# A two-block sequence model on one core: input turned before its modulation, sums shared by two engines, last norm on statistics operations

## The chip, the cores and the metric

The kernel runs on one core of a Trainium2 chip. The metric is the device time of one execution in microseconds (us). Three timed runs of the kernel before gave 2133.89 us as their median (2132.24 to 2136.08). A profile was taken of one more execution, which lasted 2128.42 us.

The engines are named as in the profile: PE is TensorE (PEld its weight loads), DVE is VectorE, ACT is ScalarE, POOL is GpSimd, SP is SyncE, which here only issues transfers.

## The reference

A sequence of 1024 tokens of 1024 features (float32) goes through two blocks. Only the two ends matter here.

```
# first block, its start
mod = silu(c) @ w_mod + b_mod               # c: (1, 1024), w_mod: (1024, 3072)
shift, scale, gate = split(mod, 3)
h = rms_norm(x, norm_g) * (1 + scale) + shift
proj = h @ w_in                             # then a state space mixer, sparse attention,
...                                         # gates, output projection, final rms_norm
# second block: projections, dilated attention, a chunked scan, two RMS norms, then its end
out = mix @ w_out                           # mix: (1024, 2048), w_out: (2048, 1024)
y = layer_norm(alpha * x + out, ln_g, ln_b) # mean and variance over 1024 features
```

In both blocks the tokens stand in 8 tiles of 128. A product with `h` wants the features on the partitions, so `x`, which arrives with tokens on the partitions, has to be transposed ("turned") on PE.

## The kernel before, in words

Every engine has its own instruction stream, written out by hand in one function, and waits on semaphores by count. SP loads the weights in 34 loads of 2 MB into two halves of one buffer `W`; a load starts when its half has been used. PE multiplies them in units of one PSUM bank, and this chain of units fills most of the span.

**The start.** SP issues, in this order, the parameters `pk`, the first half of `x` (tiles 0 to 3), the constants `ck` (they hold the identity for the transposes), `mods[0]`, the second half of `x`, `mods[1]` to `mods[3]`, and then the first two weight loads. The four `mods` are 2 MB each: 512 columns of `w_mod` for all 1024 rows of `c`; two of them land in `W` (slots 0 and 1), two in `hT`. The load of weights 0 waits until `mods[0]` has been summed (`s_macc`), the load of weights 1 until `mods[1]` has.

- DVE, function `modulation(m)` (L1731 to L1741): one multiply and seven multiply-adds of 128x512 sum `silu(c)[k] * w_mod[k]` over the eight slices k into `mod_sum[m]`. The sum over the 128 partitions is PE's: four products of 128 columns of `mod_sum[m]` with a column of ones (L1067), each a result of one column.
- ACT squares the tiles of `x` with an accumulated sum and takes the root (L1419, L1423); DVE, function `normalise(half)`, scales four tiles (L1751).
- The order on DVE is modulation 0, normalise 0, modulation 1, normalise 1, modulation 2, modulation 3. Then come three small operations that make the scale `sc1` and the shift `shf` (L1760 to L1762, the last of them signals `s_mod`).
- PE transposes 16 pieces ("turns", each four 128x128 transposes into one bank, L1057): six of them before the modulation products, ten behind them, on six banks. A turned piece is read out of PSUM by DVE (even, L1767) or ACT (odd, L1430), and this read applies `sc1` and `shf`; so none can be read before `s_mod`, and PE gets no bank for the seventh.
- The first unit of the load "small" (L868) waits for all 16 pieces. From there on PE has work.

**The end.** The last two loads, woA0 and woA1, give 16 units of 24 products each. DVE adds each unit to the row tile `res` (L2227). Behind each unit of woA1, the function `row_norm` finishes the tile before it: ACT sums the row (L1613), DVE makes the negative mean (L2212), ACT sums the squares about it (L1615), DVE makes the variance (L2214), ACT the root (L1618), and DVE the reciprocal (L2217) and three passes of 128x1024 (L2218, L1631, L2220). POOL issues the store of each tile (L770).

## Time and profile before

| what | us |
|---|---|
| median of three runs | 2133.89 |
| the profiled execution | 2128.42 |
| its span, first to last instruction | 2126.6 |
| PE busy in it | 1967.8 (93%) |
| DVE busy in it | 1157.7 (54%) |
| first unit of "small" starts on PE | 57.59 |
| last product of PE ends | 2106.13 |
| last pass of DVE ends | 2120.84 |

The page of the profile gives the shares; the times of the two ends are read from the timeline. Between 57.59 and 2106.13 PE is nearly always busy or waited for; ahead of it lies the preparation of `h`, behind it the last layer norm and its stores. The granted clock of PE is printed as a share of 2.4 GHz, so 0.50 is 1.2 GHz.

### The profile page before, as it was taken

To read this page: it belongs to the slowest core of one execution; us is meant where nothing else is said; L and a number is where in the kernel's file an instruction comes from. 1 tells how busy PE (TensorE), PEld (TensorE's weight loads), DVE (VectorE), ACT (ScalarE), POOL (GpSimd) and SP (SyncE) were. 2 spreads that over 40 slices of the span, in tenths; PEclk is the share of its full clock that TensorE was granted. 3 is DMA by queue.
4 is the path that set the end of the run, shared out by engine and by line. 5 is a ranking of instruction groups with operands and counts; after the bars stand their busy time and mean duration, and the time that the engine had idled before them with its cause. 6 is when DMAs were issued, how large, how long until landed. Compare 5 with 4: busy or idle time off the path is not lost.

```text
span 2126.6 us, 27616 instructions
## 1 busy us (share of the span) xinstructions
PE 1967.8 (93%) x10964; PEld 982.9 (46%) x10964; DVE 1157.7 (54%) x2320; ACT 757.1 (36%) x1345; POOL 613.2 (29%) x630
## 2 busy tenths in 40 slices
PE   2999889998999999989999899899999999999896
PEld 2443344454444455534444566544444444444542
DVE  6418999999995456422545688620233333332516
ACT  2413444314312866213321344331233333333503
POOL 0022415544446002478311322511101222022240
PEclk8999999999999999999999999999999999999998
DMA  8110111022311002331311100211111011100301
GB/s 336 40 45 25 50 40 50 21 85 75 129 79 69 37 11 85 139 119 40 128 40 40 40 1 1 79 40 40 41 41 41 1 41 41 41 10 32 120 20 79
DMA packets 18225, 127.10 MB, mean 60 GB/s; under 512 B 1744, under 2 KB 1744, under 8 KB 12848
## 3 DMA queue, kind: packets, MB, share of 16 engines
q1 hardware_dynamic: 12720, 97.57, 12.1%
q0 software_dynamic: 5376, 27.76, 3.3%
q8 instruction: 87, 1.43, 0.3%
q14 instruction: 42, 0.34, 0.0%
HBM read 106.45 MB, written 18.87 MB: 59 GB/s over the span
## 4 chain that ended last, share of the span: by engine, by line
PE 75%; DVE 14%; ACT 4%; POOL 3%; DMA 2%; issue 2%; SPq 0%; DVEq 0%; POOLq 0%; ACTq 0%
PE ps L871 48%; PE ps L868 7%; DVE arena L1631 3%; POOL arena L570 2%; PE ps L986 1%; PE ps L1223 1%; PE ps L921 1%; PE ps L963 1%; PE ps L969 1%; PE ps L908 1%; PE ps L1243 1%; PE ps L1088 1%; PE ps L936 1%; DMA W<-in_mods 1%; DVE arena L1847 1%
## 5 line engine op out<-in xcount | busy, mean ns | idle before, releaser
L871 PE MATMUL ps<-hT,W 128*128 128x512 bf16 x3456 | 812.3, 389 | 23.0 <-DVE arena L2150 7.2
L871 PEld LDWEIGHTS ps<-hT,W 128*128 128x128 bf16 x3456 | 327.6, 97 | 465.6 <-issue 34.9
L579 POOL TENSOR_TENSOR W<-W 128x512 bf16<-128x512 f32 x216 | 235.9, 1131 | 459.6 <-DMA W<-in_loads 458.3
L871 PE MATMUL ps<-W,arena 128*128 128x512 bf16 x1152 | 262.4, 388 | 8.8 <-DVE W L2016 6.2
L570 POOL TENSOR_TENSOR arena<-arena 128x512 f32<-128x512 f32 (+1 forms) x80 | 139.7, 1746 | 196.4 <-ACT arena L1569 126.4
L1409 ACT ACTIVATE arena<-arena,small 128x128 f32<-128x128 f32 (+9 forms) x192 | 114.1, 641 | 198.9 <-DVE small L1721 181.9
L871 PEld LDWEIGHTS ps<-W,arena 128*128 128x128 bf16 x1152 | 111.1, 97 | 158.1 <-DVE W L2016 6.7
L1402 ACT ACTIVATE arena<-arena,small 128x128 f32<-128x128 f32 (+9 forms) x192 | 122.8, 640 | 122.8 <-DVE small L1710 87.3
L868 PE MATMUL ps<-arena,W 128*128 128x512 f32 (+1 forms) x320 | 142.0, 598 | 0.9 <-DVE arena L1767 0.9
L871 PE MATMUL ps<-arena,W 128*128 128x512 bf16 x576 | 132.3, 391 | 5.4 <-POOL arena L631 4.4
L1710 DVE CUSTOM_DVE_ANT_0 arena<-ps,arena 128x256 f32<-128x256 f32 (+7 forms) x128 | 62.1, 518 | 123.8 <-PE ps L969 109.4
L741 POOL TENSOR_TENSOR small<-small 128x1024 f32<-128x1024 f32 x7 | 14.0, 1999 | 342.2 <-ACT small L1393 342.2
L1859 DVE TENSOR_SCALAR_CACHE_REDUCE small<-arena,small 128x768 bf16<-128x768 f32 (+2 forms) x93 | 101.7, 1143 | 1.1
L868 PEld LDWEIGHTS ps<-arena,W 128*128 128x128 f32 (+1 forms) x320 | 57.8, 185 | 77.9 <-issue 75.2
L871 PEld LDWEIGHTS ps<-arena,W 128*128 128x128 bf16 x576 | 55.7, 97 | 81.6 <-POOL arena L631 4.9
L871 PE MATMUL ps<-W,hT 128*128 128x512 bf16 x384 | 89.5, 388 | 0.0
L1342 ACT ACTIVATE arena<-ps 128x512 f32<-128x512 f32 x48 | 28.3, 597 | 138.2 <-PE ps L871 74.8
L1653 DVE CUSTOM_DVE_ANT_0 arena<-ps,arena 128x128 f32<-128x128 f32 (+7 forms) x64 | 45.9, 755 | 56.7 <-PE ps L921 35.9
L1683 DVE COPY arena<-ps 128x384 f32<-128x384 f32 (+2 forms) x64 | 26.3, 453 | 86.7 <-PE ps L986 46.1
L1686 DVE COPY arena<-ps 128x256 f32<-128x256 f32 (+1 forms) x64 | 30.8, 481 | 73.5 <-PE ps L989 73.5
L1640 DVE COPY arena<-ps 128x512 f32<-128x512 f32 (+3 forms) x96 | 49.0, 551 | 39.4 <-PE ps L936 39.4
L1846 DVE MAX8 small<-arena 128x8 f32<-128x384 f32 (+2 forms) x96 | 66.4, 692 | 2.1
(321 smaller groups left out, 2673.7 us busy)
## 6 DMA issues: line engine op xcount, KB each, us to landing
W<-in_loads SPq DMA_DIRECT2D x34, 2048.0 KB, 7.6
gates_scratch<-arena SPq DMA_DIRECT2D x32, 256.0 KB, 2.0
arena<-gates_scratch POOLq DMA_DIRECT2D x2, 4096.0 KB, 15.4
arena<-in_x SPq DMA_DIRECT2D x2, 2048.0 KB, 13.8
W<-in_mods SPq DMA_DIRECT2D x2, 2048.0 KB, 18.4
hT<-in_mods SPq DMA_DIRECT2D x2, 2048.0 KB, 28.8
arena<-in_x POOLq DMA_DIRECT2D x1, 4096.0 KB, 13.5
x_scratch<-arena POOLq DMA_DIRECT2D x8, 512.0 KB, 8.7
```

The source lines that it names most:

```text
L570: return nc.gpsimd.tensor_tensor(o, a, b, ALU.mult)
L579: last = nc.gpsimd.tensor_tensor(low(v), v, high(v), ALU.subtract)
L868: last = mm(o, left, right, start=(k == 0), stop=(k == steps - 1))
L871: last = mm(o, left[:, :, a], right[:, :, b], start=(k == 0 and (a, b) == PRODUCTS[0]), stop=(k == steps - 1 and (a, b) == PRODUCTS[-1]))
L1402: A(t, t, ACT.Exp, bias=mneg4[:, (n % 2) * 2 + x:(n % 2) * 2 + x + 1], scale=-1.0, accum_out=den[:, (n % 2) * 2 + x:(n % 2) * 2 + x + 1]). ...
L1409: A(t, t, ACT.Copy, scale=rden[:, (n % 2) * 2 + x:(n % 2) * 2 + x + 1]).then_inc(sems["scaled"], 1)
L1631: return V.tensor_tensor(o, a, b, ALU.mult)
L1640: V.tensor_copy(tiles["cols"][g % 2][x][:, 0:nb * P], ps[:, 6 + x, 0:nb * P]).then_inc(sems["copied"], 1)
L1653: V.tensor_tensor_reduce(tiles["rows"][n % 2][x][:, 0:keys], ps[:, 2 + 2 * x:4 + 2 * x, :].rearrange("p a b -> p (a b)")[:, 0:keys], bias_ ...
L1710: V.tensor_tensor_reduce(at2["rows"][n % 2][x][:, 0:window(i)], ps[:, 2 + at_, 0:window(i)], bias_of(items[n], x), 1.0, BIG, ALU.add, ALU.min,
L1846: link(V.max(mx, sc_at(i)))
L1859: last = V.tensor_scalar(junk[b], sc_at(i), levels[b], None, ALU.is_ge, ALU.add, accum_out=count3[:, b:b + 1])
```

## The change

SP issues the first half of `x`, then `pk`, the second half of `x`, `ck`, the four `mods` and the weights. The input is normalised, turned and copied raw out of PSUM by ACT alone, over seven banks, before any modulation; when `sc1` and `shf` are there, DVE and ACT apply them in SBUF, one 128x1024 piece for each k, and the first unit of "small" waits for its pieces one by one. Of each `mods[m]`, DVE sums 256 columns as before, and PE takes the other 256: for two column tiles, eight accumulating products of a 128x128 weight tile with one column of `silu(c)`. The loads of weights 0 and 1 wait for PE's products (`s_mcol`). In the last norm, statistics operations on DVE (one bn_stats behind each unit, one bn_aggr for each row) give mean and variance, ACT keeps only the root, and two fused passes take the place of three. SP issues the stores.

```
             def load(n):
                 ...
-                    sp.wait_ge(s_macc, n + 1)
+                    sp.wait_ge(s_mcol, n + 1)
...
+            nc.sync.dma_start(XR0[:, 0:4, :], x[0:512].rearrange("(t p) d -> p t d", p=P)).then_inc(s_x[0], 16)
             nc.sync.dma_start(pk[:], params).then_inc(s_par, 16)
-            nc.sync.dma_start(XR0[:, 0:4, :], x[0:512].rearrange("(t p) d -> p t d", p=P)).then_inc(s_x[0], 16)
+            nc.sync.dma_start(XR0[:, 4:8, :], x[512:1024].rearrange("(t p) d -> p t d", p=P)).then_inc(s_x[1], 16)
             nc.sync.dma_start(ck[:], consts).then_inc(s_con, 16)
-            nc.sync.dma_start(mod_weights(0), mods[0]).then_inc(s_modw[0], 16)
-            nc.sync.dma_start(XR0[:, 4:8, :], x[512:1024].rearrange("(t p) d -> p t d", p=P)).then_inc(s_x[1], 16)
...
+            for m in range(4):
+                nc.sync.dma_start(mod_weights(m), mods[m]).then_inc(s_modw[m], 16)
...
+            for t in range(NT):
+                sp.wait_ge(s_ln[2], t + 1)
+                nc.sync.dma_start(out[t * P:(t + 1) * P, :], res[:, t, :]).then_inc(s_out, 16)
+            sp.wait_ge(s_out, 16 * NT)
...
-            for t in range(NT):
-                pool.wait_ge(s_ln[5], t + 1)
-                nc.gpsimd.dma_start(out[t * P:(t + 1) * P, :], res[:, t, :]).then_inc(s_out, 16)
-            pool.wait_ge(s_out, 16 * NT)
...
                 for (cols, lhs, rhs), span in spans:
                     for k in span:
+                        if (name, i) == ("small", 0):
+                            pe.wait_ge(s_hta if k % 2 else s_htv, k // 2 + 1)
...
-                if n >= 6:
-                    pe.wait_ge(s_hta if n % 2 else s_htv, (n - 6) // 2 + 1)
+                if n >= 7:
+                    pe.wait_ge(s_xt_read, n - 6)
...
-            for n in range(6):
+            for n in range(16):
                 turn_input(n)
+            pe.wait_ge(s_csil, 1)
             for m in range(4):
+                pe.wait_ge(s_modw[m], 16)
+                w = mod_weights(m).rearrange("p (k n) -> p k n", k=KD)
+                for ct in range(2, 4):
+                    for k in range(KD):
+                        mm(ps[:, 0, 4 * m + ct:4 * m + ct + 1], w[:, k, ct * P:(ct + 1) * P], csil[:, k:k + 1],
+                           start=(k == 0), stop=(k == KD - 1))
                 pe.wait_ge(s_macc, m + 1)
-                for ct in range(4):
+                for ct in range(2):
                     last = mm(ps[:, 0, 4 * m + ct:4 * m + ct + 1], mod_sum[m][:, ct * P:(ct + 1) * P], ones[:, 0:1],
                               start=True, stop=True)
-            last.then_inc(s_mcol, 1)
-            for n in range(6, 16):
-                turn_input(n)
-            pe.wait_ge(s_htv, 8)
-            pe.wait_ge(s_hta, 8)
+                last.then_inc(s_mcol, 1)
             pe.wait_ge(s_mod, 1)
+            pe.wait_ge(s_xt_read, 16)
             units("small")
...
+            for n in range(16):
+                k, half = turned(n)
+                act.wait_ge(s_xt, n + 1)
+                A(h_whole[k][:, half * 512:half * 512 + 512], ps[:, 1 + n % 7, :], ACT.Copy).then_inc(s_xt_read, 1)
             A(dts, par("ldt"), ACT.Exp).then_inc(s_prm, 1)
             act.wait_ge(s_mod, 1)
-            for n in range(1, 16, 2):
-                k, half = turned(n)
-                act.wait_ge(s_xt, n + 1)
-                A(h_whole[k][:, half * 512:half * 512 + 512], ps[:, 2 + n % 6, :], ACT.Identity, scale=sc1[:, k:k + 1],
-                  bias=shf[:, k:k + 1]).then_inc(s_hta, 1)
+            act.wait_ge(s_xt_read, 16)
+            for k in range(1, KD, 2):
+                A(h_whole[k], h_whole[k], ACT.Identity, scale=sc1[:, k:k + 1], bias=shf[:, k:k + 1]).then_inc(s_hta, 1)
...
             for t in range(NT):
-                act.wait_ge(s_free, FIRST["woA1"] + t + 1)
-                ...
-                junk = row_junk[t % 2]
-                A(junk, res[:, t, :], ACT.Copy, accum_out=ss[:, t:t + 1]).then_inc(s_ln[0], 1)
-                act.wait_ge(s_ln[1], t + 1)
-                A(junk, res[:, t, :], ACT.Square, bias=nmu[:, t:t + 1],
-                  accum_out=ss2[:, t:t + 1]).then_inc(s_ln[2], 1)
-                act.wait_ge(s_ln[3], t + 1)
-                A(rss[:, t:t + 1], rss[:, t:t + 1], ACT.Sqrt).then_inc(s_ln[4], 1)
+                act.wait_ge(s_ln[0], t + 1)
+                A(rss[:, t:t + 1], rss[:, t:t + 1], ACT.Sqrt).then_inc(s_ln[1], 1)
...
-                link(V.tensor_scalar(mod_sum[m], w[:, 0, :], csil[:, 0:1], None, ALU.mult))
+                link(V.tensor_scalar(mod_sum[m], w[:, 0, 0:256], csil[:, 0:1], None, ALU.mult))
                 for k in range(1, KD):
-                    ins = V.scalar_tensor_tensor(mod_sum[m], w[:, k, :], csil[:, k:k + 1], mod_sum[m], ALU.mult, ALU.add)
+                    ins = V.scalar_tensor_tensor(mod_sum[m], w[:, k, 0:256], csil[:, k:k + 1], mod_sum[m], ALU.mult, ALU.add)
...
-            modulation(0)
             normalise(0)
-            modulation(1)
             normalise(1)
-            modulation(2)
-            modulation(3)
-            dve.wait_ge(s_mcol, 1)
+            for m in range(4):
+                modulation(m)
+            dve.wait_ge(s_mcol, 4)
...
-            for n in range(0, 16, 2):
-                ...
+            dve.wait_ge(s_xt_read, 16)
+            for k in range(0, KD, 2):
+                V.tensor_scalar(h_whole[k], h_whole[k], sc1[:, k:k + 1], shf[:, k:k + 1], ALU.mult, ALU.add).then_inc(s_htv, 1)
...
             def row_norm(t):
-                ...
+                row, mean, root = res[:, t, :], row_mean[:, t, 0:1], inv_ln[:, t:t + 1]
+                link(V.bn_aggr(row_mean[:, t, :], row_stats[:, t].rearrange("p c n -> p (c n)")))
+                V.tensor_scalar(root, row_mean[:, t, 1:2], NORM_EPS / ALPHA ** 2, None, ALU.add).then_inc(s_ln[0], 1)
+                V.scalar_tensor_tensor(row, row, mean, lng, ALU.subtract, ALU.mult)
+                dve.wait_ge(s_ln[1], t + 1)
+                link(V.reciprocal(root, root))
+                V.scalar_tensor_tensor(row, row, root, lnb, ALU.mult, ALU.add).then_inc(s_ln[2], 1)

             for u in range(FIRST["woA0"], len(UNITS)):
                 ...
                 V.scalar_tensor_tensor(v, ps[:, unit_bank(u), :], inv[:, t:t + 1], v, ALU.mult, ALU.add).then_inc(s_free, 1)
+                dve.wait_ge(s_free, u + 1)
+                link(V.bn_stats(row_stats[:, t, c, :], v))
                 ...
-                if name == "woA1" and t >= 1:
-                    row_norm(t - 1)
-            row_norm(7)
+                if c:
+                    row_norm(t)
```

Where the instructions of an engine now stand is shown at three places. PE at the very start, before: 24 transposes, 16 products with ones, the other 40 transposes, and the unit "small" (72x512). A fp32 product is one row here and two records in the trace; a transpose is one of both.

```order
L1057 MATMUL ps<-ck,arena 128x128 x24
L1067 MATMUL ps<-ck,arena 128x1 x16
L1057 MATMUL ps<-ck,arena 128x128 x40
L868 MATMUL ps<-arena,W 72x512 x16
L868 MATMUL ps<-arena,W 128x512 x16
```

PE at the same place after the change; L1071 are the new products with `silu(c)`, L1075 those with ones:

```order
L1058 MATMUL ps<-ck,arena 128x128 x64
L1071 MATMUL ps<-small,W 128x1 x16
L1075 MATMUL ps<-ck,arena 128x1 x2
L1071 MATMUL ps<-small,W 128x1 x16
L1075 MATMUL ps<-ck,arena 128x1 x2
L1071 MATMUL ps<-small,hT 128x1 x16
L1075 MATMUL ps<-ck,arena 128x1 x2
L1071 MATMUL ps<-small,hT 128x1 x16
L1075 MATMUL ps<-ck,arena 128x1 x2
L869 MATMUL ps<-arena,W 72x512 x16
```

All 64 transposes have moved ahead of the modulation; between them and "small" there now stand 72 products with one column instead of 40 transposes.

DVE at the start, before: L1735 and L1737 are `modulation`, L1747 to L1751 `normalise`.

```order
L1735 TENSOR_SCALAR arena<-W,small 128x512
L1737 SCALAR_TENSOR_TENSOR arena<-W,small,arena 128x512 x7
L1747 TENSOR_SCALAR small<-small 128x4
L1749 RECIPROCAL small<-small 128x4
L1751 TENSOR_SCALAR arena<-arena,small 128x1024 x4
```

DVE after, from its first scaling of `x` on (L1746 to L1750 are `normalise`, L1734 and L1736 `modulation`):

```order
L1746 TENSOR_SCALAR small<-small 128x4
L1748 RECIPROCAL small<-small 128x4
L1750 TENSOR_SCALAR arena<-arena,small 128x1024 x4
L1746 TENSOR_SCALAR small<-small 128x4
L1748 RECIPROCAL small<-small 128x4
L1750 TENSOR_SCALAR arena<-arena,small 128x1024 x4
L1734 TENSOR_SCALAR arena<-W,small 128x256
L1736 SCALAR_TENSOR_TENSOR arena<-W,small,arena 128x256 x7
```

Both halves of `x` come first, and the sums behind them are half as wide.

DVE in the last stage, one row tile before (from the unit's read to the last pass of the tile before it):

```order
L2227 SCALAR_TENSOR_TENSOR arena<-ps,small,arena 128x512
L2212 TENSOR_SCALAR small<-small 128x1
L2214 TENSOR_SCALAR small<-small 128x1
L2217 RECIPROCAL small<-small 128x1
L2218 TENSOR_SCALAR arena<-arena,small 128x1024
L1631 TENSOR_TENSOR arena<-arena 128x1024
L2220 TENSOR_TENSOR arena<-arena 128x1024
```

One row tile after:

```order
L2219 SCALAR_TENSOR_TENSOR arena<-ps,small,arena 128x512
L2221 BN_STATS small<-arena 128x6
L2206 BN_AGGR small<-small 128x2
L2207 TENSOR_SCALAR small<-small 128x1
L2208 SCALAR_TENSOR_TENSOR arena<-arena,small 128x1024
L2210 RECIPROCAL small<-small 128x1
L2211 SCALAR_TENSOR_TENSOR arena<-arena,small 128x1024
```

One pass of 128x1024 less stands in it, two statistics operations more, and the norm is that of the same tile, no longer of the one before.

## Rows read from the trace of the kernel before

**Rows 1.** The page: busy time, and the chain that ended last, by engine.
```profile
PE 1967.8 (93%) x10964; PEld 982.9 (46%) x10964; DVE 1157.7 (54%) x2320; ACT 757.1 (36%) x1345; POOL 613.2 (29%) x630
PE 75%; DVE 14%; ACT 4%; POOL 3%; DMA 2%; issue 2%; SPq 0%; DVEq 0%; POOLq 0%; ACTq 0%
```

**Rows 2.** Timeline of the start: start us, us, engine, instruction [idle before <-releaser].
```profile
10.21 1.06 ACT L1419 ACTIVATE arena<-arena 128x1024 bf16<-128x1024 f32 x1 [5.28 <-DMA arena<-in_x]
14.49 1.28 ACT L1423 ACT_TABLE_LOAD   x1
16.34 0.49 DVE L1735 TENSOR_SCALAR arena<-W,small 128x512 f32<-128x512 f32 x1 [11.52 <-DMA W<-in_mods]
...
22.90 2.74 DVE L1751 TENSOR_SCALAR arena<-arena,small 128x1024 f32<-128x1024 f32 x4
...
25.79 4.72 PE L1057 MATMUL ps<-ck,arena 128*128 128x128 f32 x24 [25.79 <-DVE arena L1751]
26.27 0.49 DVE L1735 TENSOR_SCALAR arena<-W,small 128x512 f32<-128x512 f32 x1 [0.62 <-DMA W<-in_mods]
...
30.34 0.95 PE L1067 MATMUL ps<-ck,arena 128*128 128x1 f32 x8
...
47.44 1.87 PE L1067 MATMUL ps<-ck,arena 128*128 128x1 f32 x8 [4.04 <-DVE arena L1737]
...
49.62 0.17 DVE L1762 SCALAR_TENSOR_TENSOR small<-small,pk 128x8 f32<-128x8 f32 x1
...
50.68 5.99 PE L1057 MATMUL ps<-ck,arena 128*128 128x128 f32 x40 [1.37 <-DVE arena L1767]
...
57.59 27.66 PE L868 MATMUL ps<-arena,W 128*72 128x512 f32 x64 [0.92 <-DVE arena L1767]
```

**Rows 3.** Timeline of the end.
```profile
2094.64 11.49 PE L871 MATMUL ps<-W,arena 128*128 128x512 bf16 x50
...
2073.53 0.75 DVE L2227 SCALAR_TENSOR_TENSOR arena<-ps,small,arena 128x512 f32<-128x512 f32 x1 [4.69 <-PE ps L871]
...
2112.19 0.81 DVE L2218 TENSOR_SCALAR arena<-arena,small 128x1024 f32<-128x1024 f32 x1
...
2119.62 1.22 DVE L2220 TENSOR_TENSOR arena<-arena 128x1024 f32<-128x1024 f32 x1
2121.14 0.53 POOL L770 DMA_DIRECT2D out<-arena  x1 [4.79 <-DVE arena L2220]
```

**Rows 4.** Landing of one early transfer: issue line, count, KB, us to landing.
```profile
W<-in_loads SPq DMA_DIRECT2D x1, 2048.0 KB, 18.6
```

**Rows 5.** Windows: span, length, busy and count by engine, then PE's granted clock.
```profile
26.30:29.70 3.40, 3.40 (x18) 3.40 (x17) 3.26 (x5) 0.51 (x2) 0.00 (x0) 1.00 1.03 439
29.70:33.10 3.40, 2.37 (x22) 2.29 (x21) 2.99 (x7) 0.70 (x2) 0.00 (x0) 1.00 1.02 434
33.10:34.00 0.90, 0.38 (x3) 0.30 (x2) 0.90 (x2) 0.89 (x2) 0.00 (x0) 0.51 0.94 400
...
54.00:55.00 1.00, 1.00 (x12) 1.00 (x11) 0.83 (x2) 0.81 (x2) 0.00 (x0) 1.00 0.06 16
```

**Rows 6.** Groups by form: line engine op, names, form, count | busy us, mean ns.
```profile
L1342 ACT ACTIVATE arena<-ps 128x512 f32<-128x512 f32 x48 | 28.3, 597 | 138.2 <-PE ps L871 74.8 <-POOL arena L701 39.0 <-POOL arena L713 17.0
L2086 DVE SCALAR_TENSOR_TENSOR arena<-arena,pk 128x1024 f32<-128x1024 f32 x36 | 48.2, 1340 | 1.3
L1859 DVE TENSOR_SCALAR_CACHE_REDUCE small<-arena,small 128x1024 bf16<-128x1024 f32 x31 | 39.5, 1275 | 0.0
L1978 DVE SCALAR_TENSOR_TENSOR arena<-arena,pk,ps 128x256 f32<-128x256 f32 x16 | 6.6, 476 | 6.3 <-PE ps L1135 6.2
```

**Rows 7.** Window of a late stage of small products, same columns.
```profile
1985.60:1992.20 6.60, 6.60 (x80) 4.09 (x76) 2.49 (x10) 3.93 (x10) 0.00 (x0) 0.50 0.01 4
```

**Rows 8.** One-column products, L1067: duration ns min/median/max, first and last start.
```profile
L1067 PE MATMUL ps<-ck,arena x32: 169/352/373, 30.3 to 49.0; 128*128 128x1 f32 x32
```

**Rows 9.** Landing of the eight stores of the end.
```profile
out<-arena POOLq DMA_DIRECT2D x8, 512.0 KB, 2.9
```

More of the change, by code:

```diff
@@ L232, in layer_kernel @@
         ident, tri, ones = con("ident"), con("tri"), con("ones")
-        mod_sum = [area(28672 + 512 * m, 512) for m in range(4)]
+        mod_sum = [area(28672 + 256 * m, 256) for m in range(4)]
         square_junk = [area(24064 + 512 * t, 512).bitcast(BF16) for t in range(4)]
@@ L308, in layer_kernel @@
                    cols=area(26624, 2048, "p (s x c) -> p s x c", s=2, x=2))
-        row_junk = [area(22528 + 1024 * s, 1024) for s in range(2)]
         y2_sum = little(1024)
         dtT = y2_sum
+        row_stats = y2_sum[:, 0:96].rearrange("p (t c n) -> p t c n", t=NT, c=2)
+        row_mean = y2_sum[:, 96:112].rearrange("p (t n) -> p t n", t=NT)
         ss = little(8)
-        ss2 = little(8)
         ssp = little(64)
@@ L427, in layer_kernel @@
         s_alibi = sem("alibi_loaded")
-        s_ln = [sem(f"layernorm_{w}") for w in ("sum", "mean", "squares", "var", "root", "row")]
+        s_ln = [sem(f"layernorm_{w}") for w in ("var", "root", "row")]
         s_out = sem("output_stored")
@@ L1053, in turn_input @@
                     pe.wait_ge(s_xn, 4 * half + 4)
-                if n >= 6:
-                    pe.wait_ge(s_hta if n % 2 else s_htv, (n - 6) // 2 + 1)
+                if n >= 7:
+                    pe.wait_ge(s_xt_read, n - 6)
                 for j in range(4):
-                    last = nc.tensor.transpose(ps[:, 2 + n % 6, j * P:(j + 1) * P],
+                    last = nc.tensor.transpose(ps[:, 1 + n % 7, j * P:(j + 1) * P],
                                                XR0[:, 4 * half + j, k * P:(k + 1) * P], ident)
@@ L1436, in _ @@
             A(r2, r2, ACT.Sin, scale=-1.0, bias=half_pi).then_inc(s_prm, 1)
-            act.wait_ge(s_htv, 8)
-            act.wait_ge(s_hta, 8)
+            act.wait_ge(s_htv, 4)
+            act.wait_ge(s_hta, 4)
             for k in range(KD):
@@ L1763, in _ @@
             dve.wait_ge(s_mod, 1)
-            for n in range(0, 16, 2):
-                k, half = turned(n)
-                dve.wait_ge(s_xt, n + 1)
-                V.tensor_scalar(h_whole[k][:, half * 512:half * 512 + 512], ps[:, 2 + n % 6, :], sc1[:, k:k + 1],
-                                shf[:, k:k + 1], ALU.mult, ALU.add).then_inc(s_htv, 1)
+            dve.wait_ge(s_xt_read, 16)
+            for k in range(0, KD, 2):
+                V.tensor_scalar(h_whole[k], h_whole[k], sc1[:, k:k + 1], shf[:, k:k + 1], ALU.mult, ALU.add).then_inc(s_htv, 1)
             dve.wait_ge(s_w[0], 16)
@@ L2210, in row_norm @@
             def row_norm(t):
-                dve.wait_ge(s_ln[0], t + 1)
-                V.tensor_scalar(nmu[:, t:t + 1], ss[:, t:t + 1], -1.0 / D, None, ALU.mult).then_inc(s_ln[1], 1)
-                dve.wait_ge(s_ln[2], t + 1)
-                V.tensor_scalar(inv_ln[:, t:t + 1], ss2[:, t:t + 1], 1.0 / D, NORM_EPS / ALPHA ** 2, ALU.mult, ALU.add)\
-                    .then_inc(s_ln[3], 1)
-                dve.wait_ge(s_ln[4], t + 1)
-                link(V.reciprocal(inv_ln[:, t:t + 1], inv_ln[:, t:t + 1]))
-                link(V.tensor_scalar(res[:, t, :], res[:, t, :], nmu[:, t:t + 1], inv_ln[:, t:t + 1], ALU.add, ALU.mult))
-                link(mult(res[:, t, :], res[:, t, :], lng))
-                V.tensor_tensor(res[:, t, :], res[:, t, :], lnb, ALU.add).then_inc(s_ln[5], 1)
+                row, mean, root = res[:, t, :], row_mean[:, t, 0:1], inv_ln[:, t:t + 1]
[5 more added lines that the diff above has]
+                V.scalar_tensor_tensor(row, row, root, lnb, ALU.mult, ALU.add).then_inc(s_ln[2], 1)
             for u in range(FIRST["woA0"], len(UNITS)):
```

10 lines of the change are left out of this document (3 added, 7 removed).

## The prediction

> **What bounds the kernel now.** I read the page first: PE is busy for 93% of the span, and the chain that ended last lies on PE for 75% of it [rows 1]. So a saving elsewhere counts only where PE has not yet begun or has already finished. The change touches just these two places. Next I read the timeline of the first 60 us. PE's first long work, the unit "small", starts at 57.59 [rows 2]. Until then it has short bursts: 24 transposes from 25.79, products with ones at 30.34 and 47.44, 40 transposes from 50.68. DVE decides: it sums until 47.4, makes the scale by 49.79, and then ten of the sixteen turns still have to be made and all sixteen read. Last I read the end: PE finishes at 2106.13, DVE at 2120.84, and the last store is issued at 2121.14 [rows 3]. The span ends at 2126.6. So 57.6 us at the start and 20.5 us at the end are open to the change, and everything between them shifts as a whole: its work, its waits and its loads all follow PE's units.
>
> **Transfers at the start.** `mods[0]` was there at 16.34 and `mods[1]` at 26.27, with the second half of x between them [rows 2]: 4096 KB in 9.93 us, 4.96 us for 2 MB. The first half of x, behind pk, was there at 10.21. The same two pieces in the other order are both there at about 10.2. ACT needs both, because its first instruction is the silu of c from pk, and so its squares begin where they began before. The second half of x follows at 15.2, ck at 16.3, and the mods at 21.2, 26.2, 31.2 and 36.1. Weights 0 were issued at 22.4 and took 18.6 us [rows 4], so they landed at 41.0, last in the queue. They are issued later now, but as long as that is before 36 they land at the same time. If PE releases them only at 38, they land near 43, still ahead of the need worked out below.
>
> **The turns.** ACT squares four tiles (10.2 to 14.7), loads its table (1.28, until 15.8 [rows 2]), and with a round trip over DVE the first scaling starts at about 16.3. It takes 2.74 us [rows 2], so PE can start at 19.1, no longer at 25.79. A transpose cost 3.40/18 = 0.19 us in the stretch behind 26.3, and 0.083 us at 54 [rows 5]. The second rate is twice the first, so PE ran at 1.2 GHz in the first and at 2.4 GHz in the second. (The granted clock of 1.00 printed for the first one stands before any recorded change of the clock, and its rate contradicts it.) The rise came 3.9 us after PE began at 25.8. So five turns go at 0.76 us, until 22.9, and three at 0.33, until 23.9. Meanwhile the second half of x is squared (16.2 to 20.5) and scaled (until 24.0). ACT copies from 21.0 on, 0.6 us each [rows 6], so copy n ends at 21.6 + 0.6n. With seven banks turn 15 needs copy 8, done at 26.4, and PE ends its turns at 26.8. ACT ends at 30.6. Both are hidden, since the last mods land at 36.1.
>
> The Trainium skill, "TensorE: Matmul & The Clock Gate", Part 4: PE-mode transpose, says that transposes do not bring the full clock. The trace disagrees: the rate doubled inside a burst of nothing but transposes [rows 5]. By the page the turns would end at 30.1, 3.3 us later.
>
> **The one-column products.** This is the term that decides the start. The change gives PE 72 of them, 144 records. A burst of 8 records took 0.95 us at 30.34 and 1.87 us at 47.44 [rows 2]: 0.12 and 0.23 us each, the first at 2.4 GHz, the second at 1.2 GHz. So the whole costs 17 us or 34 us, depending on the clock. After the last transposes at 30.5, with one-column products running from 30.34 and again from 32.32, the clock fell at 33.1, while PE was still in the second burst [rows 5]. The burst at 47.44 still ran at the lower rate. In a late stage PE was busy in all of 6.60 us with 80 small records and the clock stayed at 0.50 throughout [rows 7]. I therefore take it that the clock falls again 2.6 us behind the last transposes, at 29.4. Until then 22 records fit. The other 122 cost 0.23 at most, and less where they are not followed by a gap, since a burst of 1.87 us also holds the 0.35 us of its last record [rows 8]: (1.87-0.35)/7 = 0.217 is the lower bound. With 0.22 they take 26.8 us, until 56.2; with the two bounds 55.9 and 57.5. If the clock never rises in the turns, they end at 30.1 and the products at 30.1 + 144 x 0.234 = 63.8.
>
> DVE's sums do not bind. A 256-wide multiply-add costs 0.48 [rows 6] and 0.03 of gap, eight of them 4.0 us. Behind the scaling at 24.0 the four sums end at 28, 32, 36 and 40.1, the last bound by its landing at 36.1. The first release of weights comes at about 32.
>
> **From the products to "small".** Scale and shift took 49.79 - 49.31 = 0.5 us [rows 2]. Then one pass over 128x1024 with two scalars, 0.81 us [rows 3], frees the first product of "small", and the other pieces come faster (one every 0.5 us from two engines) than PE uses them (27.66/32 = 0.86 us at full clock [rows 2]). So "small" starts at 56.2 + 1.3 + 0.1 = 57.6, where it also started before. But now PE comes to it at 1.2 GHz. The trace shows two rises: 3.9 us after 25.8 and 2.9 us after 50.7 (53.6). Half of that is lost, 1.5 to 2.0 us; I take 1.8. Before, the transposes right ahead of "small" had paid it. The start thus comes out 1.8 us later: the 8 us that the early turns save behind the scale are eaten by the products. Its bounds are +1.2 (55.9 with 1.5) and +9.6 (63.8 + 1.4 + 2.0 - 57.6).
>
> **The end.** DVE read a unit every 5.44 us while PE bound it (0.75 of work behind 4.69 of waiting [rows 3]), and fell behind in woA1, because each row has two round trips over ACT. At PE's pace the last read would be at 2073.53 + 6 x 5.44 = 2106.17. A row now costs DVE: the read 0.75; bn_stats, which no row shows, by the nearest row, a 1024-wide operation that reduces in 1.28 [rows 6], about half, 0.7 (lower bound 0.49, a plain 512-wide pass [rows 2]; upper 1.3, two passes); bn_aggr on 12 numbers like the other tiny ones, 0.2; the variance 0.15; a fused pass of 1024, between 1.22 [rows 3] and 1.34 [rows 6], 1.3; the reciprocal 0.2, whose root from ACT is hidden under that pass; a second pass 1.3; gaps 0.25. That is 4.85 us, below 5.44, so DVE keeps up and no bank is missed. For the last row: 2106.17 + 4.85 = 2111.0 against 2120.84, which is -9.8 us; -10.3 to -8.8 with the bounds, where the upper one would also make DVE as slow as PE.
>
> The tail behind it is 2126.6 - 2120.84 = 5.8 us, of which the store takes 2.9 from issue to landing [rows 9]. SP in POOL's place: no row has a 512 KB store from SP at an idle time, so between -1 and +0.5; I take -0.3. Nothing else is queued on SP at that point, whose last load is long done, and no other instruction of POOL waited behind its stores.
>
> **Sum.** Start +1.8, end -9.8, store -0.3: -8.3 us. From the profiled execution's 2128.4 this gives 2120.1. That execution was 5.5 us below the median of the runs shown, so on the median's scale it is 2125.6.
>
> **Rivals.** *The products keep the full clock.* For it: PE will be at work without a gap from 24 to the end of the products. Against it: the fall at 33.1 and the late stage [rows 5, 7]. Then the products end at 26.8 + 17.1 = 43.9, "small" starts at 45.3 at full clock, -12.3 instead of +1.8, and the sum is -22.4: 2111.5. The Trainium skill, same page, "Why this matters for your kernels", gives this outcome by its rule that a TensorE kept busy without gaps has its full clock. By that rule the stage at 1986 should have had it, and its row shows 0.50.
>
> *The clock never rises in the turns*, because ACT's copies at 0.6 us leave PE waiting for banks. Start +9.6, end -10.1: -0.5, 2133.4. For it: PE works only about half the time from 24 to 27. Against it: from 19.1 to 23 it works without a gap, as long as before the first rise.
>
> *The products wait for each other.* Eight of them add into the same PSUM column. If each record waits for the whole of the one before, 0.35 us [rows 8], 144 x 0.35 = 50 us from 26.8: the scale is ready at 77.5, "small" at 78.4, and with 1.8 lost the start is +22.6 and the sum +12.5: 2146.4. This is slower than before from a spacing of 0.22 + 8.3/122 = 0.29 us on. Against it: the two records of one fp32 product already add into one column, and come at 0.23.
>
> *The last norm does not keep pace*, with bn_stats well over 1.3 us: DVE lags again, the end gives -3 at most, and the sum is near -1.5: 2132.4.
>
> **Chances.** Forecast 0.72, full clock 0.10, never a rise 0.09, products in series 0.05, a slow norm 0.04. The forecast alone ranges from 2122 to 2130 (its bounds and 1.5 us for comparing medians). The range that holds 8 in 10 reaches from 2115 to 2133. What can be told from no change is 0.2%, 4.3 us: faster is below 2129.6. That is nearly all of the forecast and the full clock, 0.83; the same, the slow corner of the forecast and the two cases near zero, 0.11; slower, the series and half of their upper edge, 0.06.
>
> **What would show it.** Right: turns from about 19; one-column records at 0.22 us with a clock of 0.50 from about 30 to 56; "small" from 57.6 at 1.2 GHz for its first 2 to 4 us; DVE's last pass at PE's last product plus 5 us; bn_stats near 0.7 us. Wrong: a clock of 1.00 at 40, one-column records at 0.3 us or more, a turn waiting for a bank before 24, or DVE more than one unit behind PE in woA1.

## The result, and the profile after

| | us |
|---|---|
| median of the changed kernel, four runs | 2121.33 (2120.61 to 2123.38) |
| median of the kernel before, four runs on the same chip | 2133.43 (2132.24 to 2136.08) |
| ratio | 0.9943, 95% interval 0.9926 to 0.996 |

The change saves 12.1 us, 8.5 to 16 by the interval. The profiled execution had a span of 2120.0 us, 6.6 below that of before. This table splits the span of both at the same four events, read from the timelines:

| | before | after | difference |
|---|---|---|---|
| "small" starts on PE | 57.6 | 55.4 | -2.2 |
| from there to PE's next unit of work behind "small" | 27.5 | 29.7 | +2.2 |
| from there to PE's last product | 2021.0 | 2027.3 | +6.3 |
| from there to the end of DVE's last pass | 14.7 | 4.5 | -10.2 |
| from there to the end of the span | 5.76 | 3.03 | -2.7 |

So in this pair of executions the start gave nothing, the norm gave 10.2 us, the stores 2.7, and the long middle, which the change doesn't touch, cost 6.3.

The page's first row and its chain of waits, as in [rows 1]:

```profile
PE 1995.6 (94%) x11076; PEld 1004.9 (47%) x11076; DVE 1151.7 (54%) x2324; ACT 745.1 (35%) x1325; POOL 606.3 (29%) x622
PE 80%; DVE 10%; ACT 4%; POOL 3%; DMA 2%; issue 2%; SPq 0%; DVEq 0%; POOLq 0%; ACTq 0%
```

PE is busy for 27.8 us more, of which the 128 new records of the next view make 23.7. The chain has moved to PE at both ends: in the first 58 us PE holds 38 us of it and held 8 before, and from 2040 on it holds 72 and held 34, where DVE's and ACT's row norm had been.

The timeline of the start, in answer to [rows 2]:

```profile
10.09 0.21 ACT L1418 ACTIVATE small<-pk 128x8 f32<-128x8 f32 x1 [8.09 <-DMA pk<-in_params]
16.22 2.74 DVE L1750 TENSOR_SCALAR arena<-arena,small 128x1024 f32<-128x1024 f32 x4
19.11 8.69 PE L1058 MATMUL ps<-ck,arena 128*128 128x128 f32 x64 [19.11 <-DVE arena L1750]
...
27.64 3.63 PE L1071 MATMUL ps<-small,W 128*128 128x1 f32 x32
31.58 6.16 PE L1071 MATMUL ps<-small,W 128*128 128x1 f32 x32
...
46.13 6.96 PE L1071 MATMUL ps<-small,hT 128*128 128x1 f32 x32
...
53.98 0.17 DVE L1757 TENSOR_TENSOR small<-ps,pk 128x8 f32<-128x8 f32 x1 [12.81 <-PE ps L1075]
55.42 2.80 PE L869 MATMUL ps<-arena,W 128*72 128x512 f32 x3 [1.47 <-DVE arena L1763]
```

The turns start 6.7 us earlier than before and end at 27.6. From there PE works without a gap on one-column products. The first 32 records take 3.63 us, 0.113 each. The last groups of 32 take 6.96, 0.217 each, nearly twice as long. DVE has long finished its sums and waits 12.81 us for PE. The windows, in answer to [rows 5], show the clock change inside this work (columns as there; the clock is the number ahead of the last two):

```profile
30.00:32.00 2.00, 2.00 (x20) 2.00 (x20) 1.89 (x5) 0.59 (x2) 0.00 (x0) 1.00 1.06 451
32.00:34.00 2.00, 2.00 (x14) 2.00 (x13) 1.86 (x5) 0.00 (x0) 0.00 (x0) 0.62 0.99 410
34.00:36.00 2.00, 2.00 (x11) 2.00 (x11) 1.22 (x3) 0.00 (x0) 0.00 (x0) 0.50 0.98 418
...
58.00:60.00 2.00, 2.00 (x4) 0.66 (x3) 1.67 (x10) 1.09 (x1) 0.00 (x0) 0.56 0.00 0
60.00:62.00 2.00, 2.00 (x6) 0.67 (x5) 0.61 (x4) 1.25 (x3) 0.00 (x0) 1.00 0.00 0
```

PE is busy in all of each window, and still has 2.4 GHz up to 32 and 1.2 GHz from 34 on. It gets 2.4 GHz back near 60, 4.3 us after "small" began. Half of these 4.3 us is lost, and that is the +2.2 of the second row of the table.

The end, in answer to [rows 3], the last row tile:

```profile
2112.48 0.75 DVE L2219 SCALAR_TENSOR_TENSOR arena<-ps,small,arena 128x512 f32<-128x512 f32 x1 [0.90 <-PE ps L872]
2113.26 0.69 DVE L2221 BATCH_NORM_STATS2 small<-arena 128x6 f32<-128x512 f32 x1
2113.99 0.21 DVE L2206 BATCH_NORM_AGGREGATE small<-small 128x2 f32<-128x12 f32 x1
2114.23 0.15 DVE L2207 TENSOR_SCALAR small<-small 128x1 f32<-128x1 f32 x1
2114.30 1.27 DVE L2208 SCALAR_TENSOR_TENSOR arena<-arena,small 128x1024 f32<-128x1024 f32 x1
...
2115.69 1.28 DVE L2211 SCALAR_TENSOR_TENSOR arena<-arena,small 128x1024 f32<-128x1024 f32 x1
```

DVE waits 0.90 us for this unit, so it keeps pace with PE, and it is done 4.5 us after PE's last product. The landing of the stores hardly differs from [rows 9]:

```profile
out<-arena SPq DMA_DIRECT2D x8, 512.0 KB, 2.6
```

### The profile page after: what moved, and what is told of

Read it like the earlier page. It is cut to its first block, busy times and chain, and to the rows that moved or that the text cites. A ratio compares the mean times of both kernels' runs of the same rounds, so it can differ in the third digit from the quotient of the medians.

```text
span 2120.0 us, 27820 instructions
## 1 busy us (share of the span) xinstructions
PE 1995.6 (94%) x11076; PEld 1004.9 (47%) x11076; DVE 1151.7 (54%) x2324; ACT 745.1 (35%) x1325; POOL 606.3 (29%) x622
## 4 chain that ended last, share of the span: by engine, by line
PE 80%; DVE 10%; ACT 4%; POOL 3%; DMA 2%; issue 2%; SPq 0%; DVEq 0%; POOLq 0%; ACTq 0%
PE ps L872 51%; PE ps L869 7%; DVE arena L1630 2%; POOL arena L573 2%; PE ps L1093 2%; PE ps L987 1%; PE ps L1228 1%; PE ps L922 1%; PE ps L1248 1%; PE ps L970 1%; PE ps L964 1%; PE ps L909 1%; PE ps L937 1%; PE ps L1071 1%; POOL arena L704 1%
## 5 line engine op out<-in xcount | busy, mean ns | idle before, releaser
L1652 DVE CUSTOM_DVE_ANT_0 arena<-ps,arena 128x128 f32<-128x128 f32 (+7 forms) x64 | 45.9, 755 | 62.2 <-PE ps L922 36.0
L1682 DVE COPY arena<-ps 128x384 f32<-128x384 f32 (+2 forms) x64 | 26.4, 453 | 85.8 <-PE ps L987 45.3
## 6 DMA issues: line engine op xcount, KB each, us to landing
arena<-in_x SPq DMA_DIRECT2D x2, 2048.0 KB, 10.6
hT<-in_mods SPq DMA_DIRECT2D x2, 2048.0 KB, 29.4
arena<-in_x POOLq DMA_DIRECT2D x1, 4096.0 KB, 14.5
```

Of the source, the lines that this page charges most:

```text
L1652: V.tensor_tensor_reduce(tiles["rows"][n % 2][x][:, 0:keys], ps[:, 2 + 2 * x:4 + 2 * x, :].rearrange("p a b -> p (a b)")[:, 0:keys], bias_ ...
```

## The experiments

All medians are compared with runs of the kernel before on the same chip. Its median was 2133.01 us beside the first four kernels below, 2132.83 beside the next four and 2134.12 beside the last two.

### Parts of the change alone

**The start alone** (the changed kernel with the last norm and the stores of before):

```
...
-                V.scalar_tensor_tensor(row, row, mean, lng, ALU.subtract, ALU.mult)
...
-                V.scalar_tensor_tensor(row, row, root, lnb, ALU.mult, ALU.add).then_inc(s_ln[2], 1)
...
+                link(V.tensor_scalar(res[:, t, :], res[:, t, :], nmu[:, t:t + 1], inv_ln[:, t:t + 1], ALU.add, ALU.mult))
+                link(mult(res[:, t, :], res[:, t, :], lng))
+                V.tensor_tensor(res[:, t, :], res[:, t, :], lnb, ALU.add).then_inc(s_ln[5], 1)
...
-                sp.wait_ge(s_ln[2], t + 1)
-                nc.sync.dma_start(out[t * P:(t + 1) * P, :], res[:, t, :]).then_inc(s_out, 16)
+                pool.wait_ge(s_ln[5], t + 1)
+                nc.gpsimd.dma_start(out[t * P:(t + 1) * P, :], res[:, t, :]).then_inc(s_out, 16)
```

> The start of the change alone (transfer order, raw turns, products with silu(c) on PE); the last norm and its stores as before. Theory A: the start is worth nothing. 'small' begins near 55.4 instead of 57.6, runs its first 4 us at 1.2 GHz, and PE reaches the transposes L842 at 85.1 as before; the time is that of before within 2 us. Rival B: the early start shifts the stages behind it so that they meet the clock or each other less well, and the 6 us by which PE's end moved between the two profiled executions belong to the change: 4 to 6 us slower than before. Rival C: the start is where the gain comes from: 2 us or more faster.

Measured: 2134.66 us (11 runs), ratio 1.0004, 0.9994 to 1.0014: +1.6 us in the medians, which can't be told from nothing. In its profile "small" starts at 58.9, and the work behind it at 88.1. The turns:

```profile
19.42 9.80 PE L1058 MATMUL ps<-ck,arena 128*128 128x128 f32 x64 [19.42 <-DVE arena L1758]
```

The same 64 transposes took 9.80 us here and 8.69 in the first profile. The old start varies too: in three profiled executions that have it, the work behind "small" starts at 85.1, 85.4 and 86.7; in the last of them the 40 transposes ahead of "small" took 7.47 us instead of 5.99. So by the profiles the start is worth between -1.6 and +3.0 us, and the rivals in which it decides the result fall.

**The end alone** (the kernel before with the norm and the stores of the change), and **the norm alone** (as that, with the stores issued from POOL). The lines show the second against the first:

```
...
-                sp.wait_ge(s_ln[2], t + 1)
-                nc.sync.dma_start(out[t * P:(t + 1) * P, :], res[:, t, :]).then_inc(s_out, 16)
+                pool.wait_ge(s_ln[2], t + 1)
+                nc.gpsimd.dma_start(out[t * P:(t + 1) * P, :], res[:, t, :]).then_inc(s_out, 16)
```

> The end of the change alone (statistics operations, two fused passes, stores issued by SP); the start as before. Theory A: the whole gain, 12.9 us less than before (4.5 us instead of 14.7 from PE's last product to DVE's last pass, and 3.0 instead of 5.8 from there to the end), ratio 0.994. Rival B: also 12.9 less, but then the whole change, which gained 12, should be clearly slower than this one, by 4 to 6 us. Rival C: 7 us less at most.

> As the end alone, but POOL issues the stores as before. If the stores' engine is worth what the two profiles show: 10.2 us less than before, 2.7 more than with SP's stores, with 5.8 us again between DVE's last pass and the end. If the tail got shorter for another reason (DVE and ACT less busy beside the transfers): the same time as with SP's stores.

Measured: 2120.52 (ratio 0.9936, 0.9922 to 0.9949) and 2124.03 (0.9953, 0.9941 to 0.9966), -12.5 and -9.0 us. The norm alone makes most of the gain. The stores are worth 3.5 us between the two medians, where 0.3 was forecast. The two profiles, the last pass and the stores, first with POOL, then with SP:

```profile
2112.27 1.28 DVE L2208 SCALAR_TENSOR_TENSOR arena<-arena,small 128x1024 f32<-128x1024 f32 x1
2113.85 0.53 POOL L769 DMA_DIRECT2D out<-arena  x1 [4.91 <-DVE arena L2208]
out<-arena POOLq DMA_DIRECT2D x8, 512.0 KB, 2.9
```

```profile
2116.13 1.28 DVE L2209 SCALAR_TENSOR_TENSOR arena<-arena,small 128x1024 f32<-128x1024 f32 x1
out<-arena SPq DMA_DIRECT2D x8, 512.0 KB, 2.6
```

With POOL the pass ends at 2113.55, the store is issued at 2113.85 and lands 2.9 later, near 2116.7; the span ends at 2119.3. With SP the pass ends at 2117.41, and the landing 2.6 us behind the issue brings it near 2120.0; the span ends at 2120.4. Landing differs by 0.3 us. What is left behind the landing is 2.6 us with POOL and 0.4 with SP. The kept traces also hold the records of each engine's instruction stream, which the views leave out, and these fill that time. POOL closes the program with an instruction named DRAIN. In the version with POOL's stores it comes behind the landing, from 2116.93 on, and takes 2.20 us. In the version with SP's stores POOL has it at 2051.98, right behind its last work and 68 us ahead of the end, where it takes 1.54 us and nobody waits for it; SP's own, behind the landing, takes 0.01. So of the 2.8 us between the two tails 2.2 are this instruction, 0.3 the landing, and 0.25 the issue, which follows the pass after 0.28 us on POOL and 0.03 on SP. All twelve traces agree: 2.20 us behind the last store in the three whose stores POOL issues, 1.53 to 1.54 us some 70 us ahead of the end in the other nine.

**The whole change again:**

```
(nothing edited)
```

> The whole change once more, beside its parts. Theory A: the same as the end alone within 2 us, 12 to 13 us less than before. Rival B: 4 to 6 us more than the end alone. Rival C: 5 us less than the end alone. A second profile of it also tells how far PE's end moves between executions of one kernel.

Measured: 2122.74, ratio 0.9948, 0.9935 to 0.996: -10.3 us. The end alone (-12.5) and the start alone (+1.6) add up to -10.9. In this execution the start was again the later one, "small" at 58.9:

```profile
19.45 9.76 PE L1058 MATMUL ps<-ck,arena 128*128 128x128 f32 x64 [19.45 <-DVE arena L1750]
29.04 4.52 PE L1071 MATMUL ps<-small,W 128*128 128x1 f32 x32
```

The work behind "small" starts at 88.1 in it, as in the start alone.

### Where the early turns' gain went

**The sums back to DVE** (no one-column products with `silu(c)`; DVE sums all 512 columns, PE adds the partitions):

```
...
-                for ct in range(2, 4):
-                    for k in range(KD):
-                        mm(ps[:, 0, 4 * m + ct:4 * m + ct + 1], w[:, k, ct * P:(ct + 1) * P], csil[:, k:k + 1], ...)
...
-                for ct in range(2):
+                for ct in range(4):
...
-                link(V.tensor_scalar(mod_sum[m], w[:, 0, 0:256], csil[:, 0:1], None, ALU.mult))
+                link(V.tensor_scalar(mod_sum[m], w[:, 0, :], csil[:, 0:1], None, ALU.mult))
```

> The whole change, but DVE sums all 512 columns of each piece of w_mod as before, and PE only makes the products with ones (32 records instead of 144). Theory A (the one-column products at 1.2 GHz end last at the start): DVE's sums take four times 6.0 us from 23.5 and end at 47.5, 'small' begins at 51, still at 1.2 GHz, 5 to 8 us earlier than in the whole change, and the time is 5 to 8 us less than that one's. Rival (DVE's halved sums are what made the start shorter): 'small' later than 56, and the time 2 us or more above the whole change's.

Measured: 2111.93, ratio 0.9903, 0.989 to 0.9916: -20.9 us, 10.6 more than the whole change gave in the run above (8.8 more than the 12.1 of its first series), where 5 to 8 were expected. "small" starts at 50.6, as computed, and the work behind it at 79.9, 5.2 us ahead of the changed kernel's first profile and 8.2 ahead of its second:

```profile
19.13 9.35 PE L1058 MATMUL ps<-ck,arena 128*128 128x128 f32 x64 [19.13 <-DVE arena L1744]
...
50.61 15.77 PE L869 MATMUL ps<-arena,W 128*72 128x512 f32 x32 [1.47 <-DVE arena L1757]
```

So the early turns did gain, and the products with one column had taken the gain away. The sum on DVE alone is the better half of the two.

**The same products, 128 columns wide.** The question here was whether the low clock comes with what PE is given. The column of `silu(c)` is broadcast to 128 equal columns, and one of the results is used:

```
-                        mm(ps[:, 0, 4 * m + ct:4 * m + ct + 1], w[:, k, ct * P:(ct + 1) * P], csil[:, k:k + 1],
-                           start=(k == 0), stop=(k == KD - 1))
+                        mm(ps[:, 3 + m, ct * P:(ct + 1) * P], w[:, k, ct * P:(ct + 1) * P],
+                           csil[:, k:k + 1].to_broadcast([P, P]), start=(k == 0), stop=(k == KD - 1))
...
+                last = V.tensor_copy(mod_cols[:, 4 * m:4 * m + 4],
+                                     ps[:, 3 + m, :].rearrange("p (c w) -> p c w", c=4)[:, :, 0])
```

> The whole change with one size changed: the moving operand of the 64 new products is the same column of silu(c) read 128 times (a broadcast), so that each result is 128 equal columns, of which DVE copies one (4 tiny copies more, about 1 us). Same weight loads, same count. Theory A (the clock falls behind the last wide work, whatever PE's busy time): the clock stays at 1.00 through the products, a record comes every 0.12 to 0.16 us, the products end by 48, 'small' begins by 50 at full clock, and the time is 7 to 11 us less than the whole change's. Rival (the clock falls because of the weight loads, or of fp32 products): clock 0.50 again from about 31, 0.21 us or more a record, 'small' at 56 to 60, the same time.

Measured: 2110.13, ratio 0.9893, 0.9879 to 0.9908: -22.7 us, 12.4 more than the whole change in the run above, where 7 to 11 were expected.

```profile
28.12 3.74 PE L1073 MATMUL ps<-small,W 128*128 128x128 f32 x32
40.10 3.82 PE L1073 MATMUL ps<-small,hT 128*128 128x128 f32 x32
45.94 20.34 PE L870 MATMUL ps<-arena,W 128*72 128x512 f32 x43 [1.68 <-DVE arena L1769]
```

```profile
28.10:44.30 16.20, 16.16 (x146) 16.07 (x144) 10.74 (x27) 2.90 (x5) 0.00 (x0) 1.00 1.00 426
48.00:49.00 1.00, 1.00 (x2) 0.24 (x1) 0.90 (x6) 1.00 (x2) 0.00 (x0) 0.50 0.00 0
```

The clock is 1.00 through all 16.2 us of the products, and 32 records take 3.74 to 3.82 us instead of 6.96. The share of busy time was 100% in both kernels, and the count of records is the same. A product with 128 times the columns costs the same at 2.4 GHz as the one-column product at its best (0.117 against 0.113), and half of it at its worst. Behind the products PE has a gap of 1.7 us, and in "small" the clock still dips to 0.50 near 48.

**`silu(c)` as the weights and 256 columns of `w_mod` as the moving operand**, so that one record does what two did; the result is a row, which ACT copies and PE turns back into columns:

```
-                for ct in range(2, 4):
-                    for k in range(KD):
-                        mm(ps[:, 0, ...], w[:, k, ct * P:(ct + 1) * P], csil[:, k:k + 1], ...)
...
+                for k in range(KD):
+                    last = mm(ps[0:1, 3 + m, 0:256], csil[:, k:k + 1], w[:, k, 256:512], start=(k == 0), stop=(k == KD - 1))
...
+                A(mod_row[0:1, 256 * m:256 * m + 256], ps[0:1, 3 + m, 0:256], ACT.Copy).then_inc(s_mrc, 1)
```

> The whole change with the operands of the new products exchanged: silu(c) is the weight (one column) and 256 columns of w_mod move, 8 products a piece instead of 16, each result a row on one partition, which ACT copies and PE turns by two products with a single one. Theory A: 256 moving columns hold the clock at 1.00; 16 records of 0.21 us and 6 to 8 small ones a piece, 4 us, so that DVE's last sum at 41.2 ends last and 'small' begins at 43 to 45 at full clock: 12 to 16 us less than the whole change. Rival (a weight of one column does not hold the clock): 16 records of 0.43 us and the small ones at 0.23, 8 us a piece, 'small' at 58 or later, the same time within 2 us.

Measured: 2114.86, ratio 0.9915, 0.9902 to 0.9928: -18.0 us, 7.7 more than the whole change in the run above. The clock held at 1.00 through the products, but 12 to 16 us more were expected, with "small" at 43 to 45.

```profile
27.89 7.07 PE L1088 MATMUL ps<-W,small 128*1 128x256 f32 x32
...
47.79 18.73 PE L873 MATMUL ps<-arena,W 128*72 128x512 f32 x37 [1.47 <-DVE arena L1781]
```

```profile
27.90:45.00 17.10, 17.10 (x88) 8.07 (x88) 10.78 (x23) 4.33 (x9) 0.00 (x0) 1.00 0.98 417
45.00:48.00 3.00, 1.53 (x12) 1.44 (x12) 1.58 (x5) 1.17 (x2) 0.00 (x0) 0.72 0.03 11
```

A record with 256 columns takes 7.07/32 = 0.22 us, so half as many records cost about as much as the 128-column ones. The way back into columns comes on top, and in it PE is idle for half of the stretch from 45 to 48; "small" starts at 47.8 with the clock already falling.

**The old order of the transfers**, with the rest of the change:

```
-            nc.sync.dma_start(XR0[:, 0:4, :], ...).then_inc(s_x[0], 16)
-            nc.sync.dma_start(XR0[:, 4:8, :], ...).then_inc(s_x[1], 16)
             nc.sync.dma_start(pk[:], params).then_inc(s_par, 16)
+            nc.sync.dma_start(XR0[:, 0:4, :], ...).then_inc(s_x[0], 16)
             nc.sync.dma_start(ck[:], consts).then_inc(s_con, 16)
-            for m in range(4):
+            nc.sync.dma_start(mod_weights(0), mods[0]).then_inc(s_modw[0], 16)
+            nc.sync.dma_start(XR0[:, 4:8, :], ...).then_inc(s_x[1], 16)
+            for m in range(1, 4):
```

> The whole change with the transfers in their old order (pk, first half of x, ck, first mods, second half of x, the other mods). The second half of x lands at 21.4 instead of 15.2. Theory A: PE stands idle between the two halves of the turns and turns the second half at 1.2 GHz until 35, the products follow at 1.2 GHz until 63 to 66, 6 to 10 us above the whole change. Rival (the order is hidden by the products' own wait for the mods): within 2 us of the whole change.

Measured: 2127.49 (7 runs), ratio 0.9971, 0.9959 to 0.9982: -5.3 us, 5.0 less than with `x` first. That lies between the 6 to 10 us that were expected and the rival's 2. The second half of the turns waits for its tiles and runs until 34.0, and everything behind it is late:

```profile
29.01 5.11 PE L1059 MATMUL ps<-ck,arena 128*128 128x128 f32 x32 [1.85 <-DVE arena L1751]
...
61.79 2.80 PE L870 MATMUL ps<-arena,W 128*72 128x512 f32 x3 [1.47 <-DVE arena L1764]
```

### Putting it together

**A filler ahead of "small".** To the 128-wide kernel, 16 transposes are added that start when the last column product is out and run while DVE makes the scale. Nobody uses their results.

```
+            pe.wait_ge(s_xt_read, 14)
+            for j in range(16):
+                nc.tensor.transpose(ps[:, 7, (j % 4) * P:(j % 4 + 1) * P], XR0[:, j % 8, 0:P], ident)
```

> The wide products, with 16 transposes more on PE (their result is not used) behind the last product, where PE waits for the scale. In the profile of the wide products the clock stood at 1.00 until 47.5, fell there for some 2 us, behind a gap of 1.7 us and the slow entry into 'small', and rose again. Theory A (this dip is the price of the gap): the filled gap keeps the clock at 1.00 through the first unit of 'small', and L842 is reached at 27.6 us after the unit's start, 1.5 us earlier than without the filling. Rival (the dip comes from the products with one column ahead of it or at random): the same dip, no gain.

Measured: 2109.47, ratio 0.9887, 0.9872 to 0.9902: -24.7 us, against -22.7 without the filler; the two intervals overlap.

```profile
45.40 1.95 PE L1082 MATMUL ps<-ck,arena 128*128 128x128 f32 x16
47.21 3.19 PE L870 MATMUL ps<-arena,W 128*72 128x512 f32 x7
```

```profile
48.00:50.00 2.00, 2.00 (x6) 0.71 (x5) 1.93 (x7) 2.00 (x3) 0.00 (x0) 1.00 0.00 0
```

The dip is gone: the clock is 1.00 at 48 to 50, and from the start of "small" to the work behind it are 27.5 us, the time of before, instead of 29.2. The turns ended 1.3 us later in this execution, which hides the gain in the profile's total. In the medians the filler's 2.0 us are not clear of noise; the stage's own time is what shows it.

**The best version: the wide products, the filler, and the first `mods` summed by DVE alone,** so that PE's products start with the second one:

```
...
-            for m in range(4):
...
+            wide(1)
+            with_ones(0)
+            with_ones(1)
+            for m in (2, 3):
+                wide(m)
+                with_ones(m)
```

> The wide products and the filling, and of the first piece of w_mod DVE sums all 512 columns, since it stands idle for 2 us ahead of the last piece; PE makes 48 wide products instead of 64. PE's last product then ends at 41.9 instead of 44.3, 'small' begins at 43.5, 2.4 us earlier than with the wide products, and the time is about 2 to 4 us less than theirs, 25 us less than before: 2106 to 2108. Rival: DVE's longer first sum makes PE wait for the ones product and the clock falls again: no gain or a loss of 2 us.

Measured: 2105.29 (2103.28 to 2106.65), ratio 0.9868, 0.9851 to 0.9884: -28.8 us, just past the 2106 to 2108 that were expected. It beats both kernels: the changed one gave -10.3 and -12.1 in its two series.

```profile
28.88 3.74 PE L1074 MATMUL ps<-small,W 128*128 128x128 f32 x32
...
42.00 1.94 PE L1093 MATMUL ps<-ck,arena 128*128 128x128 f32 x16
43.81 2.77 PE L870 MATMUL ps<-arena,W 128*72 128x512 f32 x6
```

```profile
28.90:44.00 15.10, 15.01 (x135) 14.83 (x134) 13.62 (x34) 3.90 (x6) 0.00 (x0) 1.00 0.98 404
```

"small" starts at 43.8 and the work behind it at 71.3, 13.8 us ahead of before. With the end's 12.5 that is 26.3; the medians say 28.8. The filler and DVE's longer first sum were not tried without the wide products.

## Why the prediction was right, and where it was off

The forecast was 2125.6, and the median is 2121.33: inside the stated range of 2115 to 2133, and just under the 2122 to 2130 that the forecast's own bounds gave. The place of each gain and loss was right; two sizes were off.

- **The turns.** First scaling at 16.3 by the forecast, 16.22 measured; PE from 19.1, measured 19.11; end at 26.8, measured 27.6 (29.1 in two other executions, where 64 transposes took 9.8 us and not 8.7). Right.
- **The one-column products.** This is the term that decided the start, and its mechanism held: the clock fell in the middle of them and stayed at 0.50, with a record at 0.217 us where 0.22 was taken. The fall was put at 29.4 and came between 32 and 34. So more records ran at 0.113 us, and "small" could start 2.2 us earlier than forecast. That the low clock goes with these products is shown by the wide version of them, which kept 1.00 at the same busy share and count.
- **The loss in "small"** was taken as 1.8 and measured as 2.2. With the earlier scale the start is 0.0 in the first profile, where +1.8 stood. In the later two it was +3.0 against the same profile of before, and +1.6 in the medians of the start alone. The bounds, +1.2 to +9.6, were too high at their lower end.
- **The norm** was sized at -9.8 and measured at -10.2. bn_stats takes 0.69 where 0.7 was taken from half of a 1024-wide reduction, bn_aggr 0.21 for 0.2, the fused passes 1.27 and 1.28 for 1.3. The last row took 4.5 us behind PE, not 4.85.
- **The stores** are the mis-sized term: -0.3 was taken, and -2.7 is measured in the profiles (5.76 to 3.03 and 5.75 to 2.99), 3.5 between the medians of the two versions. The step that failed: of the 5.8 us behind the last pass, 2.9 are the landing [rows 9], and only these were priced for the new issuer. The other 2.9 were left as they were, though 2.5 of them hung on POOL: its closing DRAIN of 2.2 us behind the landing, and 0.25 of the issue. Even the lower bound of -1 missed it.
- **The sum.** -8.3 was forecast. The two medians of the whole change say -12.1 and -10.3. By the measured terms it is the start's -1.6 to +3.0, then -10.2 and -2.7, so -14.5 to -9.9.
- **Two slips in the working**, on which neither the forecast nor its range hangs. At 0.19 us each the 64 transposes end at 31.2 and not at 30.1, so the upper bound of the start and the rival in which the clock never rises are 1.1 us too low. And the chances of the forecast and of the full clock add up to 0.82, so "faster" could not have 0.83.

The profiled pair alone would mislead: -6.6, since the middle took 2021.0 us in the one and 2027.3 in the other. In twelve profiled executions it went from 2021.0 to 2027.9: up to 2027.5 in the three with the old start, from 2022.5 in the nine with a new one. By the traces' record of it, the granted clock was 0.50 for 78.5 us of this stretch before and for 95.6 us after, 17 us more, of which half at most is lost. The shortest of the twelve middles had the least time at 0.50, and the longest, 2027.9, had 95.6 us too. But four executions with 85.3 us at 0.50 took from 2023.2 to 2027.5 us, so the clock is not shown to be all of it. One place of it, a block of 384 equal products far from both ends, first before, then after:

```profile
1420.58 86.58 PE L871 MATMUL ps<-W,arena 128*128 128x512 bf16 x384 [2.03 <-DVE arena L2166]
```

```profile
1420.00:1460.00 40.00, 39.42 (x176) 16.85 (x177) 0.52 (x1) 4.82 (x7) 8.03 (x8) 1.00 0.11 44
```

```profile
1424.71 88.19 PE L872 MATMUL ps<-W,arena 128*128 128x512 bf16 x384 [2.03 <-DVE arena L2160]
```

```profile
1424.00:1464.00 40.00, 39.29 (x168) 16.55 (x169) 0.65 (x1) 4.13 (x6) 8.04 (x8) 0.96 0.11 46
```

The same block behind the same idle time of 2.03 us takes 1.6 us longer, and the granted clock is 0.96 there and not 1.00. It is the clock then, in this block: 0.04 of the 40 us is 1.6. Why it fell in one execution and not in the other stays open. The profiled execution of before, which the forecast saw 5.5 us under its median, had the shortest middle of the twelve.

Of the rivals, the one with the full clock came true only once the products were made wide: "small" then starts at 45.9, where this rival had 45.3, though the clock dips afterwards. The Trainium skill's rule behind it ("TensorE: Matmul & The Clock Gate", "Why this matters for your kernels"), that a TensorE kept busy without gaps runs at its full clock, fails on the changed kernel's own row: busy 2.00 of 2.00 with 0.50, from 34 on. The products in series fall by 0.217 us a record, since that rival decided only from 0.29. The norm out of pace falls by the 0.90 us that DVE waits for its last unit. The clock that never rises in the turns falls by 64 transposes in 8.69 us: at the 0.19 of the lower rate they would have taken 12. The same page's Part 4, which says that transposes do not bring the full clock, is contradicted by this too, for the float32 transposes of this kernel.

## What to carry to other kernels

Before work is moved to PE, look up what it does to the clock, not only how many records it has: here one-column products ran at half rate though PE was never idle, took back all that the earlier turns had saved, and handed the next stage a low clock. The same products with a broadcast operand 128 columns wide cost 0.12 us a record, as the one-column ones do at their best, and kept 2.4 GHz; they took more room in PSUM and four tiny copies. And split the tail of a kernel into landing and what follows it before it is priced: the second part was 2.6 us with POOL as the issuer of the last store and 0.4 us with SP, because POOL's closing DRAIN then came 68 us before the end and not behind the landing.

## What the runs showed of the hardware that was not expected

- A store of 512 KB lands in 2.9 us from POOL and 2.6 from SP, but the span ends 2.6 us behind the landing with POOL's and 0.4 with SP's. POOL's closing DRAIN takes 2.20 us behind its own stores and 1.54 us behind its last sum.
- At an equal busy share of 100% the granted clock was 0.50 with records of 128x1 and 1.00 with records of 128x128 or 128x256, float32 in all three.
- Equal blocks of PE work in the same program differ by 1.6 us in 87 between executions, with the granted clock at 0.96 and 1.00.
- In twelve executions the stretch that no version changed varied by 6.9 us, more than half of what the change is worth. A term of a few us has to be read at its own place or from medians.
